# Four seams of a fused two-block kernel: when a stage's operand and weights are split, and which stages share a block

## What is computed

```python
# first block: the head, and the end of attention
h = rmsnorm(x, norm_mix_g);  proj = h @ w_in
y = sigmoid(g_a) * (o_a @ w_o_a) + sigmoid(g_b) * (o_b @ w_o_b)
x = x + y @ w_out
# the seam: final norm of block one, input norm of block two
x = x + moe(rmsnorm(x, norm_ffn_g))
x = rmsnorm(x, final_norm_g)
h = layer_norm(concat([meta, x]), ln_in_g, ln_in_b)
p = h @ w_in_2                      # conv_in is its first part
# second block: the MLP at the end
u = causal_dwconv(h @ ffn_up, ffn_dw)
h = layer_norm(ALPHA * h + (silu(u[..., D_FF:]) * u[..., :D_FF]) @ ffn_down, ln2_g, ln2_b)
```

## Time and profile before

| | |
|---|---|
| median of 3 runs | 2231.27 us (2227.53 to 2238.28) |
| the profiled execution | 2231.33 us |
| its span | 2229.6 us |
| PE busy, and weight loads | 1988.4 us (89%), 1689.8 us (76%) |
| DVE, ACT, POOL busy | 1311.2 (59%), 945.0 (42%), 711.1 us (32%) |

### The profile page before, as it was taken

One profiled execution on the slowest core, in us unless ns is written; L12 is line 12 of the kernel. 1 busy time (PEld: TensorE's weight loads), 2 busy tenths in 40 slices (PEclk: granted clock), 3 DMA queues, 4 the chain that ended last, 5 costly groups with the idle time before them and its releaser, 6 DMA issues. The chain is left out here.

```text
span 2229.6 us, 36859 instructions
## 1 busy us (share of the span) xinstructions
PE 1988.4 (89%) x14734; PEld 1689.8 (76%) x14734; DVE 1311.2 (59%) x1946; ACT 945.0 (42%) x1485; POOL 711.1 (32%) x378
## 2 busy tenths in 40 slices
PE   6999998799799997598999796688899989999797
PEld 4777644575677776598999575688689979999684
DVE  3779645432789897505999475565421167887402
ACT  4234258523788887522222543233333153232322
POOL 2433300131121111143433164421135425555441
PEclk9999988899899999699999897799789999999899
DMA  4222210022999998223223013210132212222231
GB/s 175 86 78 92 67 48 1 29 85 77 369 350 370 353 364 301 86 87 121 88 86 134 29 48 99 45 31 13 40 115 93 78 57 95 88 93 86 70 100 38
DMA packets 89378, 260.09 MB, mean 117 GB/s; under 512 B 26304, under 2 KB 27472, under 8 KB 88464
## 3 DMA queue, kind: packets, MB, share of 16 engines
q1 hardware_dynamic: 85488, 247.90, 32.1%
q0 software_dynamic: 3744, 10.11, 1.3%
HBM read 239.10 MB, written 18.87 MB: 116 GB/s over the span
## 5 line engine op out<-in xcount | busy, mean ns | idle before, releaser
L1546 DVE TENSOR_TENSOR moe_wlo<-moe_ring,moe_whi 128x1024 fp32r<-128x1024 f32 x198 | 234.0, 1219 | 43.4 <-ACT moe_whi L1542 40.5
L528 PE MATMUL acc<-h_xhi,h_whi 128*128 128x264 f32 x816 | 234.5, 287 | 13.1 <-DVE h_xlo L463 7.2
L528 PE MATMUL acc<-h_xlo,h_whi 128*128 128x264 f32 x816 | 233.5, 286 | 0.0
L528 PE MATMUL acc<-h_xhi,h_wlo 128*128 128x264 f32 x816 | 233.3, 286 | 0.0
L1542 ACT ACTIVATE moe_whi<-moe_ring 128x1024 fp32r<-128x1024 f32 x198 | 203.6, 1058 | 37.2 <-PE acc L1602 19.2
L528 PE MATMUL acc<-ff_xhi,ff_whi 128*128 128x258 f32 x704 | 200.8, 285 | 9.4 <-DVE ff_xlo L463 9.4
L528 PE MATMUL acc<-ff_xhi,ff_wlo 128*128 128x258 f32 x704 | 199.8, 284 | 0.0
L528 PE MATMUL acc<-ff_xlo,ff_whi 128*128 128x258 f32 x704 | 199.7, 284 | 0.0
L395 POOL TENSOR_TENSOR h_wlo<-ring,h_whi 128x1024 fp32r<-128x1024 f32 x49 | 117.5, 2400 | 201.7 <-ACT h_whi L387 201.7
L528 PEld LDWEIGHTS acc<-h_xhi,h_whi 128*128 128x128 f32 x816 | 156.1, 191 | 14.4 <-DVE h_xlo L463 8.3
L1986 DVE SCALAR_TENSOR_TENSOR acc<-cp,par,acc 128x528 f32<-128x528 f32 x232 | 159.2, 765 | 0.0
(11 more groups left out here) (506 smaller groups left out, 5158.4 us busy)
## 6 DMA issues: line engine op xcount, KB each, us to landing
ring<-slabs SPq DMA_DIRECT2D x213, 512.0 KB, 3.4
moe_ring<-moe_slabs SPq DMA_DIRECT2D x204, 512.0 KB, 5.7
tok_rows<-h_tok SPq DMA_DIRECT2D x5, 512.0 KB, 4.3
h_spill<-x2r SPq DMA_DIRECT2D x1, 2112.0 KB, 6.6
v_spill<-rw_v SPq DMA_DIRECT2D x1, 2112.0 KB, 7.4
y_spill<-cp SPq DMA_DIRECT2D x8, 264.0 KB, 4.6
rw_v<-v_spill SPq DMA_DIRECT2D x1, 2112.0 KB, 8.1
x2r<-h_spill SPq DMA_DIRECT2D x1, 2112.0 KB, 8.4
```

The costliest lines, as they stand in the source:

```text
L528: mm = nc.tensor.matmul(acc[j][0:rows, s, 0:t1 - t0], wp[:, at:at + rows], xp[:, t0:t1], start=(k == 0 and m == 0), stop=(k == kt - 1 and ...
L1546: tensor_tensor(wlo[u % AHEAD][:, :], ringm[u % RAW][:, :], whi[u % AHEAD][:, :].bitcast(F32), ALU.subtract).then_inc(w_lo[u % 2], 1)
```

## The change

1. **Head.** The weights' buffers for `w_in` are made before the norm, and the norm's block splits slabs 0 and 1 of `c_q`: ScalarE rounds slab 0 after the squares and slab 1 after the root, GpSimd subtracts.
2. **Out projection.** `out_projection` is gone; its work stands in the block of `w_o_a` and `w_o_b`. ScalarE rounds the sum's tiles among the last slabs, VectorE subtracts four of them between its last products and four behind them.
3. **Seam.** The product with the gain goes to tiles of its own (`ent_y`), so it waits only for the sum; the step that needs L760's result is a function `easing` behind it. The gain's row and the meta rows are loaded by SyncE in the experts' block, behind its first twelve slabs, into the room of `xt`, which is free there. ScalarE and GpSimd split slabs 0 and 1 of `conv_in` in the seam's block; the two subtractions on VectorE and two roundings leave the next block.
4. **MLP.** `ffn_down` is computed in the block of `ffn_up`. The first 8 tiles of `ff_hid` are split during `ffn_up` (one rounding and one subtraction for each second up tile, from tile 7 and tile 9 on), the other 14 after it, over the room of `ffn_up`'s operand and weights.

The diff, cut to its core:

```diff
@@ normalize @@
-                        if split:
+                        if split and not enter:
...
+                        if split and enter:
+                            split[0].act(act, split[0].ahead(split[1])[0])
                         wait(act, sq_used, kt)
                         nc.scalar.activation(fold(std[:, :], t), A(1, t), ACT.Sqrt,
                                              bias=k0("eps", 1, eps)).then_inc(rooted, 1)
+                        if split and enter:
+                            split[0].act(act, split[0].ahead(split[1])[1])
@@ first_block @@
+                    in_w = Weights(in_ctx, "in", side="right")
                     normalize("mix", lambda k: xt[:, k, :], lambda k: h[:, k, :], KD, T1, k0("mean1024"),
-                              None, left=mix_rstd, enter=(load, arrived))
+                              None, left=mix_rstd, enter=(load, arrived), split=(in_w, "c_q"))
...
+                gain, xm = xt[:, 0:2, :].rearrange("p a t -> p (a t)"), xt[0:META, 2:4, :].rearrange("p a t -> p (a t)")
+                def for_seam(sp):
+                    sp.dma_start(gain, final_row.to_broadcast([P, D])).then_inc(gain_in, 16)
+                    sp.dma_start(xm, meta_rows).then_inc(meta_in, 16)
@@ enter_second @@
-                    sp.dma_start(xm[:, :], meta_rows).then_inc(meta_in, 16)
-                    sp.dma_start(gain[:, :], final_row.to_broadcast([P, D])).then_inc(gain_in, 16)
...
                     nc.clear_and_free_semaphores(first_sems)
+                    for n in first_slabs:
+                        w.pool(pool, n)
...
                     nc.scalar.activation(dummy[:, :], k0("eps", 1, EPS_RMS), ACT.Sqrt)
+                    for n in first_slabs:
+                        w.act(act, n)
...
                         v.tensor_tensor(x[t][:, :], x[t][:, :], x1[:, t, :], ALU.add).then_inc(added, 1)
+                        dve.wait_ge(added, t + 1)
+                        L(v.tensor_tensor_reduce(y[t][:, :], x[t][:, :], gain, 1.0, 0.0, ALU.mult, ALU.add, one(total, t)))
+                        v.tensor_scalar(one(minus, t), one(total, t), -1.0 / D, None, ALU.mult).then_inc(gained, 1)
+
+                    def easing(t):
                         dve.wait_ge(squared, t + 1)
-                        L(v.tensor_tensor_reduce(x[t][:, :], x[t][:, :], gain[:, :], 1.0, 0.0, ALU.mult, ALU.add, one(total, t)))
-                        v.tensor_scalar(one(minus, t), one(total, t), -1.0 / D, None, ALU.mult).then_inc(gained, 1)
                         v.tensor_scalar(one(ease, t), one(sq, t), EPS_OF_LN / D, EPS_OF_LN * EPS_OF_RMS, ALU.mult, ALU.add).then_inc(eased, 1)
...
                     for t in range(4):
                         scaled(t)
+                        easing(t)
                         if t:
                             normal(t - 1)
@@ attention_part, last block @@
                     pe_tiles(pe, w, "w_o_b", 4, KD, bx, T1, oy_ready, oy_out, first=8)
+                    pe_tiles(pe, w, "w_out", KD, KD, yx, T1, xo_ready, xo_out, then=behind, prior=(oy_out, 16))
...
+                    for j, slab in enumerate(slab_range("w_o_b") + w.ahead("w_out")):
+                        w.act(act, slab)
+                        while n < min(2 * j - 3, KD):
+                            summed(n)
+                            n += 1
+                    for k in range(n, KD):
+                        summed(k)
...
                         if i >= 9:
                             both(i - 9)
+                        if i >= 12:
+                            yx.low(dve, i - 12)
                     both(7)
+                    for k in range(4, KD):
+                        yx.low(dve, k)
@@ mixers, block of conv_in @@
-                        w.act(act, first_slabs[0])
...
-                        w.dve(dve, first_slabs[0])
                         dve.wait_ge(meta_hi, 1)
...
-                            if q == 4:
-                                w.dve(dve, first_slabs[1])
@@ ffn @@
                         pe_tiles(pe, w, "ffn_up", KD, 2 * NF, hx, T3, up_ready, up_read)
+                        pe_tiles(pe, wd, "ffn_down", NF, 8, dx, T1, dn_ready, dn_out, prior=(up_read, 2 * NF))
...
                             if i % 2 and i >= 3:
-                                silu(act, i // 2 - 1)
+                                silu(i // 2 - 1)
+                                if 0 <= i // 2 - 3 < EARLY:
+                                    round_hid(i // 2 - 3)
+                            if i >= 2 * NF - 3 and i < 2 * NF - 1:
+                                wd.act(act, down[i - 2 * NF + 3])
                         tile_loop(act, w, [("ffn_up", KD, 2 * NF)], take)
-                        for n in wd.ahead("ffn_down"):
+                        for f in range(EARLY, NF):
+                            if f == NF - 4:
+                                silu(NF - 1)
+                                wd.act(act, down[2])
+                            round_hid(f)
...
+                            if i % 2 and 0 <= i // 2 - 4 < EARLY:
+                                dx.low(dve, i // 2 - 4)
+                        for f in range(EARLY, NF):
+                            dx.low(dve, f)
```

More of the change, by code:

```diff
@@ L698, in enter_second @@
             with ExitStack() as ex, block() as b:
-                x = [sbt(ex, f"ent_x{t}", [P, D]) for t in range(4)]
-                xm, gain = sbt(ex, "ent_meta", [META, D]), sbt(ex, "ent_gain", [P, D])
-                spare, spare_m = [sbt(ex, f"ent_spare{i}", [P, D]) for i in range(2)], sbt(ex, "ent_spare_meta", [META, D])
+                rows = lambda n: nc.alloc_sbuf_tensor_at(n, [P, D], F32, offset=at + 4 * D * next(place))
+                place = itertools.count()
+                x, y = [rows(f"ent_x{t}") for t in range(4)], [rows(f"ent_y{t}") for t in range(4)]
+                spare, spare_m = [rows(f"ent_spare{i}") for i in range(2)], rows("ent_spare_meta")[0:META, :]
                 total, minus, sq, var, ease, root = (sbt(ex, "ent_" + n, [P, 4]) for n in ("total", "minus", "sq", "var", "ease", "root"))
@@ L776, in _ @@
                     dve.wait_ge(m_centred, 1)
[L777 removed]
+                    v.tensor_scalar(xm, xm, of_meta[:, 1:2], of_meta[:, 3:4], ALU.add, ALU.mult).then_inc(m_normed, 1)
                     dve.wait_ge(gain_in, 16)
@@ L791, in normal @@
                         dve.wait_ge(gained, t + 1)
-                        v.tensor_scalar(x[t][:, :], x[t][:, :], one(minus, t), one(root, t), ALU.add, ALU.mult).then_inc(normed, 1)
+                        v.tensor_scalar(y[t][:, :], y[t][:, :], one(minus, t), one(root, t), ALU.add, ALU.mult).then_inc(normed, 1)
                     for t in range(4):
                         scaled(t)
+                        easing(t)
                         if t:
@@ L1091, in attention_part, with tally, behind @@
                 ax.start(lambda k: oa[:, k, :])
                 bx.start(lambda k: ob[:, k, :])
+                yx.start(lambda k: h[:, k, :])
                 @b.tensor
                 def _(pe):
+                    def tally(k):
+                        o = PCOL["router"] + 40 * k
+                        pe.wait_ge(gained, k + 1)
+                        nc.tensor.matmul(acc[0][0:40, 1, :], par[:, o:o + 40], h[:, k, :], start=(k == 0), stop=(k == KD - 1))
+                        pe.wait_ge(squared, k + 1)
+                        nc.tensor.matmul(acc[1][64:96, 1, :], k0("mean1024", 32), sq[k % 4][:, :], start=(k == 0),
+                                         stop=(k == KD - 1)).then_inc(tallied, 1)
+                    def behind(i):
+                        if i >= 2:
+                            tally(i - 2)
@@ L1101, in _ @@
                     w.begin(act, ["w_o_a"], ax, bx)
-                    w.all_act(act, ["w_o_a", "w_o_b"])
-                    for n in w.ahead("w_out"):
-                        w.act(act, n)
+                    w.all_act(act, ["w_o_a"])
+                    n = 0
+                    for j, slab in enumerate(slab_range("w_o_b") + w.ahead("w_out")):
[3 more added lines that the diff above has]
+                            n += 1
@@ L1120, in _ @@
                             both(i - 9)
+                        if i >= 12:
+                            yx.low(dve, i - 12)
                     both(7)
-                    dve.wait_ge(y_sum, 8)
-                @b.gpsimd
-                def _(pool):
-                    w.all_pool(pool, ["w_o_a", "w_o_b"])
-                    for n in w.ahead("w_out"):
-                        w.pool(pool, n)
-                @b.sync
-                def _(sp):
-                    load_slabs(sp, "w_o_b")
@@ L1186, in _ @@
                 def _(pool):
-                    w.all_pool(pool, ["w_out"])
+                    w.all_pool(pool, ["w_o_a", "w_o_b", "w_out"])
                 @b.sync
@@ L3254, in _ @@
                                 w.pool(pool, n)
-                            if f == NF - 1:
```

(3 more changed lines are left out.)

197 lines of the change are left out of this document (86 added, 111 removed).

## The result

The changed kernel takes 2205.28 us (median of 4 runs, 2201.07 to 2211.33), the kernel before beside it 2229.4 (2225.58 to 2238.28): ratio 0.9895, 95% interval 0.9856 to 0.9935. The forecast was 2208, in a range of 2197 to 2217. The profiled execution of the changed kernel is the lowest of the four, 2201.07 us, its span 2199.3 us against 2229.6. So it shows 30.3 us won where the medians show 24. That gap is one of the things to explain.

A forecast was written before the change was run, and what follows sets the result against it. PE standing still at stage meetings, with cold clock starts and GpSimd holds on VectorE, was taken as the bound. 3.8 + 3.3 + 2.0 + 6.1 + 8.0 = 23.2 us off 2231.33 gave 2208 us, range 2197 to 2217.

The forecast's parts named there:

- What bounds it: Whole kernel: PE is busy 89% of 2229.6 us; time is won only at its stops, lengthened by cold clock and GpSimd holds.
- The head: First tile: GpSimd's two slab steps no longer hold VectorE, 1.9 + 2.15 - 0.3 = 3.8 us won (0 to 4.1).
- The out projection: Start of `w_out`: no meeting of engines, but one 2.2 us hold and a third of a cold start; 3.3 us won (2.0 to 6.6).
- The seam's front: Seam up to its last normalization: 4.0 us earlier, less 2.0 for the held meta rows' normalization; 2.0 us won (0 to 4.0).
- The start of `conv_in`: ScalarE's start to last k's matmul: subtractions, waits and a hold gone (5.1), PE's second stop (1.0); 6.1 us won (4.5 to 7).
- The MLP: `ffn_up` to first `ffn_down` tile: 11.29 us stop replaced by two short ones, 2.1 us cold clock; 8.0 us won (5 to 13.8).
- the load in the experts: Experts' block: gain and meta row loads moved there from the seam cost 0, at most 5.7 us.
- the added steps in `ffn_up`: `ffn_up`: eight added roundings and subtractions cost 0, up to 5 us if each also meets a hold.
- The slower rival: `ffn_up`: added subtractions push VectorE over 11.5 us a pair, 34 us lost, 2243 us in all; chance 0.04.
- Holds don't bite: All four places: short steps slip in between GpSimd's, PE stays warm; 33 us won, 2198 us; chance 0.20.
- The seam's front gives nothing: Seam: ScalarE's two roundings and `easing` keep VectorE waiting, last normalization no earlier; 2210 us; chance 0.10.
- The split chain stays the bound: All places: VectorE still late, every short stop costs a full cold start; 14.5 us won, 2217 us; chance 0.16.

The follow-up runs named there:

- run 3: Changed kernel, with slab 1 of `w_out` subtracted by VectorE behind its chain, not by GpSimd; last `w_o_b` product to first `w_out` result 6.24 us instead of 8.40.
- run 4: Changed kernel, with slab 1 of `conv_in` subtracted by VectorE in `conv_in`'s block, not by GpSimd in the seam; experts' end to last normalization 22.67 us instead of 24.53.
- run 1: Kernel before, with only the six input projection weight buffers moved to the right side of SBUF; 2236.58 us, ratio 1.0023 to the kernel before.
- run 6: Changed kernel with 16 `hid` tiles split early instead of 8, the subtraction's result in the place of `hid`; 2204.88 us, ratio 0.9888 to the kernel before.
- run 5: Changed kernel with no `hid` tile split early, the subtraction's result in the place of `hid`; last `ffn_up` copy to first `ffn_down` result 26.43 us instead of 21.04.

## Why the prediction was right, point by point

- **What bounds it** (PE standing still at four meetings, cold starts, holds): right. Each of the four terms was in the trace at its place.
- **The head, 3.8 us:** measured 3.66; in all nine kernels with the early split the first copy came between 31.86 and 33.16. Both holds are gone and the reciprocal was not held. The five kernels with the old head had it between 36.03 and 37.54, so on the mean of the profiles the gain is 4.5 (36.95 less 32.48). This term and `conv_in`'s are read from the traces; no run undoes them one by one.
- **The out projection, 3.3 us:** 3.80 in the profile, 2.2 to 3.8 over the profiles. The mechanism is shown (run 3). The cold clock after a stop of 2.4 us, of which I charged a third (0.8), is really a coin: nothing, or 1.3 to 1.5 us.
- **The seam's front, 2.0 us:** 3.35. The mechanism is shown (run 4: the hold costs 1.86 us, 2.0 were charged), the size was off, by 1.35 us, in two terms. The first product came 9.58 us after the end of the experts, where my readings amount to 10.3 (896.3 less 886.0): 0.1 of this is the hold, 0.5 the meta rows, which are done earlier than I put (in run 4, without the hold, the first sum starts 6.49 us after the experts' end, and I had 893.0, or 7.0). And the way from the first product to the last normalization took 14.95 us (892.57 to 907.52), where I had put 15.6.
- **The start of `conv_in`, 6.1 us:** 5.24. PE lost its second stop and the held subtractions as forecast, but PE still began at 1.2 GHz. Over the nine profiles with the change the way from the block's start to the first sigmoid is 16.5 to 18.0 us, against 22.8 in the five without; the share of the cold start that I credited (1.0 us) comes in some of them.
- **The MLP, 8.0 us:** 7.96 in the profile, 9.5 in two others where the clock stayed up. I had two stops of 1 and 2.4 us, there were three, 3.6 us in all; the 2.1 us of cold clock that I added are, like the out projection's, a coin: 1.6 us or nothing. The parts, which I had not separated: merging 2.6, early splits 5.4.
- **Taken at nothing: the load in the experts.** The experts' stretch was 396.7 to 397.0 us in the five kernels with the old loads, and 396.5 to 399.5 in the nine with the loads of gain and meta rows behind the first twelve slabs. From the last reduction of the routing (`rt_cnt`) to the first product with `hid_t_hi` it is 35.5 to 35.9 us in the former and 35.7 to 37.3 in the latter. So about 1 us on the mean (397.9 against 396.9), within the bound of 5.7, not 0. No run moves the two loads alone; that they are the cause is likely and not shown.
- **Taken at nothing: the added steps in `ffn_up`:** right, 247.65 against 247.69 us, and with twice as many steps 247.68. The slower rival is dead.
- **Missing from the sum: the weight buffers' new place,** +5.5 us in the input projections. The step that failed is "What is taken at nothing": it goes through added loads and steps, and leaves out that operands which nobody recomputes change their addresses, which is a term of 5.5 us (run 1). It was neither in the sum nor in a bound. In the medians most of it was set off by stretches with unchanged code, the middle above all (877.1 us on the mean of five profiles made from before, 873.3 on that of nine made from after); how much of that is luck and how much comes with the shifted times can't be told from so few, and stays open.
- **The rivals.** "Holds don't bite" falls with runs 3 and 4. "The seam's front gives nothing" falls: the sums follow at 3.57 us. "The split chain stays the bound" was right in its first half only: in the MLP VectorE's chain is the bound still (run 6 took 5.4 us out by shortening it), but the short stops cost no full cold start (1.6 us at most, not 2.3).

## What to carry to other kernels

Put the same events of two traces beside each other, unchanged stretches too: only that showed that 5.5 us of 24 were paid back in code that nobody had touched. An allocation that moves (another side, another row stride) is a part of a change and has a price; where PE is busy all the time, count its matmuls in a window of fixed length. An early split pays until PE no longer stops. And where GpSimd's step on a slab that isn't needed yet falls into VectorE's last chain, VectorE can do it behind that chain: 2.2 us in run 3, 1.9 in run 4.

A single profiled execution of this kernel can be off by 10 us through the clock alone, more than most single edits are worth. The terms have to be read in their own stretch. There they repeat within 0.1 us as long as the granted clock is the same, and differ by up to 1.6 us where it is not.

## What the runs showed of the hardware that I had not expected

- **Matmuls of one shape have no fixed duration.** With PE never waiting and the clock at 2.4 GHz, 40 us held 177, 175 or 172 of them, depending on where the weights lie. 32 bytes more or less changed it; a shift by 1024 bytes did not.
- **After a pause PE can stay at 1.2 GHz for a long time though it is busy.** Some 19 us in the group norm of before, at a busy share of 100% (every other group of its matmuls reads 16 partitions only), and some 8 us in the same place of another kernel's profile. The Trainium skill (TensorE: Matmul & The Clock Gate, Part 1: The HAM clock gate) says that the number of slow matmuls at a start differs from run to run of the same kernel; the traces agree, in the middle of a kernel too (after a stop of 2.40 us nothing or 1.3 to 1.5 us, after a pause of 4.4 us 8 or 19 us).
- **Which engine is held isn't settled by who comes into whose run.** In run 5 a GpSimd product came into VectorE's back-to-back subtractions and waited for all that were left: 8.51 us for 1.3 us of work, while VectorE went on at 0.61 us each. My "the two engines take turns, whole instructions at a time" was wrong there. It is the only such wait in the 14 profiles, though. In the changed kernel the same product came into such a run at 2050.17 and took 1.32 us, and VectorE's next subtraction was held (1.79 us instead of 0.68). What decides between the two is open.
